# Four elementwise passes of the first norm moved from the DVE to the Pool, in a decoder layer with expert retrieval

## The chip, the cores and the metric

One core of a Trainium2 chip runs the whole kernel. The metric is device time in microseconds, the median of three runs. DVE is the vector engine, Pool is GpSimd, ACT is the scalar engine, PE is TensorE, SP issues plain DMAs.

## The reference

One decoder layer over 256 tokens of width 2048, in float32: a token mixer (recurrence and latent attention) and then an expert-retrieval feed-forward. Only the place between the two is touched:

```
x = layer_norm(DN_ALPHA * x + (1 + gt1) * mixed, ln1_g, ln1_b)   # first norm
h = x * (1 + sc2) + sh2
q = (h @ w_q)                         # 8 heads x 2 halves of 128
s = q . sub_keys; top 16 of each half; top 16 of the 16 x 16 sums -> 16 experts per token and head
act = gelu(h . expert_u[idx]) * softmax(best)
y  = sum over 8 heads x 16 experts of act * expert_v[idx]
x = layer_norm(DN_ALPHA * x + (1 + gt2) * y, ln2_g, ln2_b)
```

`expert_u` and `expert_v` have 16384 rows of 2048 floats. Each token tile of 128 tokens fetches 8 x 16 rows per token of each table.

## The kernel before, in words

Tokens lie in two tiles of 128 (T = 0, 1). After the first norm `x1[T]` holds the normalised residual without its gain and shift. Two things are derived from it on the DVE: `h2[T] = x1[T] * mods[2] + mods[1]` (the expert input, with the norm's rows folded into the two `mods` rows; lines 1775 and 1778), and the residual itself, `x1[T] = x1[T] * ln1[0] + ln1[1]` (lines 1781 and 1784; two multiplies and two additions of 128x2048). The residual is only read again by `finish(0)` and `finish(1)`, hundreds of microseconds later. PE has by then read `x1` for its transposes (semaphore `h2T_done`).

PE meanwhile multiplies with `peer_wq` in 16 weight units of four column blocks (`query_unit`), with `scores(b)` after the first unit of the next block. `scores(1)` waits until ACT has copied the queries of block 1 out of PSUM (`query(1)`), which stands on ACT behind `weigh(0, 0, 0)`, and this behind the DVE's first four dot products. The scores of head 0, tile 0, come out of the first half block early, so that the ranking can begin.

`topk(H)` on the DVE is the ranking of one head of one tile: `top_halves`, `top_pairs` (line 1741 is the 16 x 16 sum), `experts` (lines 1756, 1760, 1762 and 1764 turn ranks into row numbers; 1764 signals `topk_ok`), `expert_gates`.

The Pool issues every gather, in a written order, one indirect DMA per expert, 128 rows of 8 KB (1 MB) each. Head 0's 16 `u` gathers go to the slots in `first_u = (2, 3, 0, 1, 4, 2, 3, 5, 0, 1, 6, 4, 7, 5, 6, 7)`. Slots 0 and 1 lie where `ln1[0]` and `ln1[1]` lie, so before the change gather 2 waits until the DVE has run the four passes (`dots_done` raised by 8). Slots 4 to 7 wait for PE to be done with a weight unit (`unit_used`), a slot used again waits for its dot product (`dots_done`). Then come `first_v` (slots that lie on later weight units), and the loops of `u_group` and `v_group`, four gathers behind one small index copy (line 482): a `u` group waits for the DVE's dot products, a `v` group for PE's products (`pv_done`). The DVE's dot product of an expert is line 1807 (head 0) or 1820 (all others). It ranks head 1 after the second dot of head 0, and head 2 after the first four dots of head 1.

Of the kernel before, what the change touches and what calls it, by code (L numbers as in the profile page):

```python
# [12 lines left out]
ALU = mybir.AluOpType  # L13
# [6 lines left out]
NT = S // P  # L20
# [26 lines left out]
GROUP = 4  # L47
# [53 lines left out]
def build(nc, t, out):  # L101
    with ExitStack() as ctx:
        def sem(name):
            return ctx.enter_context(nc.semaphore(name))
# [16 lines left out]
        def at(off, n):  # L121
            return arena[:, off:off + n]
# [91 lines left out]
        x1 = [at(W + D * i, D) for i in range(NT)]  # L214
# [40 lines left out]
        ln1 = [at(R_HG, D), at(R_HG + D, D)]  # L255
# [16 lines left out]
        in_wg, in_x2, in_ln1, in_ln2, in_keys = (sem(n) for n in ("in_wg", "in_x2", "in_ln1", "in_ln2", "in_keys"))  # L272
# [24 lines left out]
            "xc_ok", "gates_done", "gates_out", "tanh_ok", "sqrt_ok", "gelu_in", "gelu_ok", "hg_ok", "in_gate_ok"))  # L297
        mod_done, mod_ok, mix_ok = (sem(n) for n in ("mod_done", "mod_ok", "mix_ok"))
        keys_t, keys_ok = sem("keys_t"), sem("keys_ok")
        var_ok, std1_ok, h2_ok, h2T_done, h2T_out = (sem(n) for n in ("var_ok", "std1_ok", "h2_ok", "h2T_done", "h2T_out"))  # L300
        sc_done, sc_out, stage_ok, best_ok, gexp_ok, topk_ok, zero_ok = (sem(n) for n in (
            "sc_done", "sc_out", "stage_ok", "best_ok", "gexp_ok", "topk_ok", "zero_ok"))
        shift_ok, norm_ok = sem("shift_ok"), sem("norm_ok")
# [2 lines left out]
        dots_done, z_ok, a_ok, diag_ok, pv_done, y_done = (sem(n) for n in ("dots_done", "z_ok", "a_ok", "diag_ok", "pv_done", "y_done"))  # L306
# [138 lines left out]
        @block.gpsimd  # L445
        def _(pool):

            me = Chain(pool, pool_s)
            pool.wait_ge(rope_ok, 1)
            for i in range(4 * KT):  # L450
                if i >= 3:
                    pool.wait_ge(mod_used, i - 2)
                pool.dma_start(ada_raw[i % 3], ada_v[:, i % KT:i % KT + 1, 2 * D + 1024 * (i // KT):2 * D + 1024 * (i // KT + 1)].rearrange("p t c -> p (t c)")  # L453
                               ).then_inc(in_ada[i % 3], 16)

            def ada_load(n, kt):
                pool.wait_ge(mod_used, n * KT + (4 * KT + kt - 3))
                pool.dma_start(ada_raw2[kt % 4], ada_v[:, kt:kt + 1, bass.ds(n * 1024 + 4 * D, 1024)].rearrange("p t c -> p (t c)")  # L458
                               ).then_inc(in_ada2[kt % 4], 16)

            pool.wait_ge(h_oout, HEADS)
            with pool.Fori(0, 4) as n:
                for kt in range(KT):
                    ada_load(n, kt)

            for e in range(TOPK):
                s = first_u[e]
                if e == 0:
                    pool.wait_ge(topk_ok, 1)
                elif s == 0 and e < 4:  # L470
                    pool.wait_ge(dots_done, 2 * GROUP)
                elif s in first_u[:e]:
                    pool.wait_ge(dots_done, 2 * GROUP + first_u.index(s) + 1)
                elif s >= 4:
                    pool.wait_ge(unit_used, 4 * B_WQ + s + 2)
                pool.indirect_dma_start(uslot[s], None, t["peer_u"][0], bass.IndirectOffsetOnAxis(arena[:, o_idx + e:o_idx + e + 1].bitcast(U32), 0)
                                        ).then_inc(in_u[s], 16)

            def index_group(ix, H, e):

                pool.sem_inc(pool_gate, 1)
                me.do(pool.tensor_copy(ix[:, e % 8:e % 8 + GROUP], arena[:, bass.ds(H * TOPK + (o_idx + e), GROUP)].bitcast(U32)))  # L482
                me.wait()
                pool.sem_inc(pool_gate, 1)

            def u_group(H, ahead, q):

                e = ahead * TOPK + q * GROUP
                if q == 0:
                    pool.wait_ge(topk_ok, H + (ahead + 1))  # L490
                pool.wait_ge(dots_done, H * TOPK + (e + GROUP))
                index_group(idxu, H, e)
                for s in range(e % 8, e % 8 + GROUP):
                    pool.indirect_dma_start(uslot[s], None, t["peer_u"][0], bass.IndirectOffsetOnAxis(idxu[:, s:s + 1], 0)).then_inc(in_u[s], 16)  # L494

            def v_group(H, q):

                e = q * GROUP
                pool.wait_ge(pv_done, H * TOPK + (e + GROUP))
                index_group(idxv, H, e)  # L500
                for s in range(e % 8, e % 8 + GROUP):
                    pool.indirect_dma_start(vslot[s], None, t["peer_v"][0], bass.IndirectOffsetOnAxis(idxv[:, s:s + 1], 0)).then_inc(in_v[s], 16)  # L502

            def first_v(s):

                pool.wait_ge(unit_used, 4 * B_WQ + (10, 12, 13, 14, 15, 16, 16, 16)[s])
                pool.indirect_dma_start(vslot[s], None, t["peer_v"][0], bass.IndirectOffsetOnAxis(arena[:, o_idx + s:o_idx + s + 1].bitcast(U32), 0)
                                        ).then_inc(in_v[s], 16)

            first_v(0)  # L510
            u_group(0, 1, 0)
            for s in (1, 2, 3):
                first_v(s)
            u_group(0, 1, 1)
            for s in (4, 5, 6, 7):
                first_v(s)
            for q in (2, 3):
                u_group(0, 1, q)
                v_group(0, q)
            last = NT * PH - 1  # L520
            with pool.Fori(1, last - 2) as H:
                me.enter(H, 1, 2 * TOPK // GROUP)
                for q in range(TOPK // GROUP):
                    u_group(H, 1, q)
                    v_group(H, q)
            me.leave(last - 3)
            u_group(last - 1, 0, 0)
            v_group(last - 2, 0)
            v_group(last - 2, 1)
            u_group(last - 1, 0, 1)  # L530
            v_group(last - 2, 2)
            u_group(last - 1, 0, 2)
            v_group(last - 2, 3)
            v_group(last - 1, 0)
            u_group(last - 1, 0, 3)
            v_group(last - 1, 1)
            u_group(last, 0, 0)
            v_group(last - 1, 2)
            v_group(last - 1, 3)
            u_group(last, 0, 1)  # L540
            v_group(last, 0)
            u_group(last, 0, 2)
            v_group(last, 1)
            u_group(last, 0, 3)
            v_group(last, 2)
            v_group(last, 3)
# [710 lines left out]
        def _(dve):  # L1257
            me = Chain(dve, dve_s)
            V = dve
            TT, TS, STT = V.tensor_tensor, V.tensor_scalar, V.scalar_tensor_tensor  # L1260
# [260 lines left out]
            for h in range(HEADS):  # L1521
                g, n = h // 4, h % 4
# [183 lines left out]
            def topk(H):  # L1706
                top_halves(H)
                top_pairs()
                experts(H)
                expert_gates(H)  # L1710
# [63 lines left out]
            for T in range(NT):  # L1774
                me.do(TT(h2[T], x1[T], mods[2], ALU.mult))
            me.wait()
            for T in range(NT):
                me.do(TT(h2[T], h2[T], mods[1], ALU.add))
            topk(0)
            for T in range(NT):  # L1780
                me.do(TT(x1[T], x1[T], ln1[0], ALU.mult))
            me.wait()
            for T in range(NT):
                me.do(TT(x1[T], x1[T], ln1[1], ALU.add))
            dve.wait_ge(h2T_out, 4)
            V.memset(zeros, 0.0).then_inc(zero_ok, 1)
            me.wait()
# [51 lines left out]
            def finish(T):  # L1839

                for c in range(4):
                    dve.wait_ge(y_done, 4 * T + c + 1)
                    cs = slice(512 * c, 512 * (c + 1))
                    me.do(TT(h2[T][:, cs], ps[:, 4 * T + c, :], mods[3][:, cs], ALU.mult))
                    me.wait()
                    me.do(STT(x1[T][:, cs], x1[T][:, cs], ALPHA, h2[T][:, cs], ALU.mult, ALU.add))
                    me.wait()
                    me.do(V.bn_stats(bn6[T][:, c, :], x1[T][:, cs]))
                if T:
                    normalized_last()  # L1850
                    return
                scale_of(T, T + 2)
                me.wait()
                for c in range(4):
                    cs = slice(512 * c, 512 * (c + 1))
                    dve.wait_ge(norm_ok, 4 * NT + 4 * T + c + 1)
                    me.do(TT(x1[T][:, cs], x1[T][:, cs], ln2[0][:, cs], ALU.mult))
                    me.wait()
                    TT(x1[T][:, cs], x1[T][:, cs], ln2[1][:, cs], ALU.add).then_inc(ln2_ok, 1)
# [9 lines left out]
            dots(PH + 1, 1, True)  # L1869
            dve.wait_ge(in_ln2, 32)  # L1870
            dve.wait_ge(mod_ok, 4)
            finish(0)
            loop(PH + 2, NT * PH - 1, 1)
            dots(NT * PH - 1, 1, False)
# [20 lines left out]
```

## Time and profile before

| | |
|---|---|
| median of 3 runs | 2408.27 us (2407.72 to 2410.21) |
| the profiled execution | 2410.57 us, its span 2408.9 us |
| PE busy | 2084.0 us (87%) |
| DVE busy | 1487.2 us (62%) |
| POOL busy | 775.6 us (32%) |
| ACT busy | 576.8 us (24%) |
| DMA queue of the Pool (gathers, and loads of w_ada) | 604.02 MB, 61.6% of 16 engines' span |

An engine's busy time says how long it had an instruction running, not that it set the pace. Where the DMA share is 1 over a long stretch, the bytes set it.

### The profile page before, as it was taken

How to read it: one execution, taken by the hardware profiler on the slowest of the kernel's cores; microseconds unless marked ns; L12 is line 12 of the kernel's file. 1: busy time of each engine (PE TensorE's matmuls, PEld its weight loads, DVE VectorE, ACT ScalarE, POOL GpSimd, SP SyncE). 2: the span in 40 equal slices, each digit the busy share in tenths (PEclk: the TensorE clock that was granted, in tenths of full speed). 3: DMA queues.
4: the chain of work that ended last, by engine and by line, in shares of the span. 5: the costliest groups of instructions: out<-in, count | busy, mean ns of one | idle time of the engine just before them, and what ended most of it. 6: DMA issues, size and time to landing. Idle time of an engine off the chain costs nothing.

```text
span 2408.9 us, 26246 instructions
## 1 busy us (share of the span) xinstructions
PE 2084.0 (87%) x9124; PEld 1428.6 (59%) x9124; DVE 1487.2 (62%) x2122; ACT 576.8 (24%) x1102; POOL 775.6 (32%) x766
## 2 busy tenths in 40 slices
PE   4899898899989999989978787877887778888887
PEld 4788798898989998878633333333333333333333
DVE  5736657657867656568665566656666765566344
ACT  1013452553334333321211111111111221111101
POOL 0000010100111000005566545554454555454662
PEclk8899899999999999999988988988898898889998
DMA  9976665754988765578999999999999999999996
GB/s 357 384 225 201 215 223 176 265 201 157 356 284 293 267 208 195 192 252 325 407 422 421 422 422 421 422 422 422 422 421 421 422 422 422 422 422 422 422 407 267
DMA packets 216162, 809.92 MB, mean 336 GB/s; under 512 B 24824, under 2 KB 45968, under 8 KB 149520
## 3 DMA queue, kind: packets, MB, share of 16 engines
q0 software_dynamic: 92160, 604.02, 61.6%
q1 hardware_dynamic: 123264, 204.11, 24.9%
q8 instruction: 55, 0.90, 0.1%
q10 hardware_dynamic: 656, 0.66, 0.1%
q14 instruction: 27, 0.22, 0.0%
HBM read 806.64 MB, written 2.10 MB: 336 GB/s over the span
## 4 chain that ended last, share of the span: by engine, by line
PE 47%; DMA 18%; DVE 15%; issue 8%; POOL 6%; ACT 4%; SPq 1%; DVEq 0%; POOLq 0%; ACTq 0%
PE ps L551 47%; DMA front<-in_peer_u,arena 13%; DVE front L1820 3%; DVE arena L1820 2%; DMA arena<-in_peer_u,arena 2%; POOL front L502 2%; DVE arena L1344 1%; POOL arena L502 1%; POOL arena L494 1%; DMA arena<-in_w_ada 1%; POOL front L494 1%; DMA front<-in_w_ada 1%; SPq L335 1%; POOL arena L482 1%; DMA arena<-in_peer_v,arena 1%
## 5 line engine op out<-in xcount | busy, mean ns | idle before, releaser
L551 PE MATMUL ps<-arena 128*128 128x512 f32 (+4 forms) x2190 | 648.7, 450 | 129.1 <-ACT arena L1170 95.1
L551 PE MATMUL ps<-front,arena 128*128 128x512 f32 (+1 forms) x1344 | 636.2, 632 | 121.9 <-ACT arena L1170 121.9
L551 PEld LDWEIGHTS ps<-arena 128*128 128x128 f32 (+1 forms) x2190 | 381.0, 201 | 384.4 <-issue 238.6
L551 PEld LDWEIGHTS ps<-front,arena 128*128 128x128 f32 x1344 | 274.6, 207 | 478.1 <-issue 354.9
L1820 DVE CUSTOM_DVE_ANT_0 arena<-arena 128x2048 f32<-128x2048 f32 x120 | 274.2, 2294 | 272.1 <-DMA arena<-in_peer_u,arena 271.8
L1820 DVE CUSTOM_DVE_ANT_0 front<-front,arena 128x2048 f32<-128x2048 f32 x120 | 274.0, 2292 | 194.8 <-DMA front<-in_peer_u,arena 193.4
L551 PE MATMUL ps<-split_f,split_ring 128*128 128x256 f32 x896 | 259.4, 290 | 0.0
L1497 DVE TENSOR_TENSOR split_ring<-front,split_pada 128x2048 fp32r<-128x2048 f32 x72 | 164.9, 2292 | 128.1 <-ACT split_pada L1077 127.7
L1158 ACT ACTIVATE arena<-arena 128x4 f32<-128x4 f32 x64 | 13.3, 207 | 960.7 <-DVE arena L1800 960.7
L453 POOL DMA_DIRECT2D arena<-in_w_ada x64 | 34.2, 535 | 517.8 <-DVEq L1409 198.6
L551 PE MATMUL ps<-arena,front 128*128 128x256 f32 (+1 forms) x864 | 190.4, 380 | 10.3 <-DVE front L1593 6.2
L482 POOL COPY arena<-arena 128x4 uint32 (+1 forms) x122 | 90.0, 738 | 334.0 <-PE ps L551 333.7
L1077 ACT ACTIVATE split_pada<-front 128x2048 fp32r<-128x2048 f32 x70 | 134.0, 1914 | 257.8 <-PE ps L551 257.8
L502 POOL DMA_INDIRECT front<-in_peer_v,arena x155 | 166.6, 1075 | 66.1 <-issue 41.0
L551 PEld LDWEIGHTS ps<-arena,front 128*128 128x128 f32 x864 | 164.6, 198 | 33.3 <-DVE front L1593 6.3
L551 PE MATMUL ps<-split_ht,split_pada 128*128 128x256 f32 x640 | 181.9, 284 | 0.0
L551 PEld LDWEIGHTS ps<-split_f,split_ring 128*128 128x128 f32 x896 | 178.4, 199 | 0.0
L494 POOL DMA_INDIRECT front<-in_peer_u,arena x120 | 151.2, 1260 | 52.1 <-issue 28.6
L494 POOL DMA_INDIRECT arena<-in_peer_u,arena x120 | 149.6, 1247 | 53.5 <-issue 28.7
L551 PEld LDWEIGHTS ps<-split_ht,split_pada 128*128 128x128 f32 x640 | 123.5, 193 | 0.0
L502 POOL DMA_INDIRECT arena<-in_peer_v,arena x93 | 108.4, 1166 | 44.0 <-POOL arena L482 25.1
L458 POOL DMA_DIRECT2D arena<-in_w_ada x64 | 33.9, 530 | 241.2 <-DVE front L1593 102.2
(259 smaller groups left out, 2892.1 us busy)
## 6 DMA issues: line engine op xcount, KB each, us to landing
front<-in_w_in SPq DMA_DIRECT2D x68, 1024.0 KB, 7.2
arena<-in_w_ada POOLq DMA_DIRECT2D x128, 512.0 KB, 6.0
front<-in_w_ada SPq DMA_DIRECT2D x64, 512.0 KB, 7.8
front<-in_w_rnn_out SPq DMA_DIRECT2D x16, 1024.0 KB, 5.6
front<-in_w_mla_out SPq DMA_DIRECT2D x16, 1024.0 KB, 5.2
front<-in_w_o SPq DMA_DIRECT2D x16, 1024.0 KB, 5.1
front<-in_peer_wq SPq DMA_DIRECT2D x13, 1024.0 KB, 6.5
arena<-in_w_ukv SPq DMA_DIRECT2D x16, 512.0 KB, 6.0
```

The lines of the kernel that those rows point to most:

```text
L335: sp.dma_start(ring[s].rearrange("p (t h c) -> p t h c", t=2, h=2)[:, :, h, :], ada_g[:, bass.ds(i * 8 + 2 * s, 2), h, j, :]).then_inc(in_ ...
L453: pool.dma_start(ada_raw[i % 3], ada_v[:, i % KT:i % KT + 1, 2 * D + 1024 * (i // KT):2 * D + 1024 * (i // KT + 1)].rearrange("p t c -> p ...
L458: pool.dma_start(ada_raw2[kt % 4], ada_v[:, kt:kt + 1, bass.ds(n * 1024 + 4 * D, 1024)].rearrange("p t c -> p (t c)")).then_inc(in_ada2[kt ...
L482: me.do(pool.tensor_copy(ix[:, e % 8:e % 8 + GROUP], arena[:, bass.ds(H * TOPK + (o_idx + e), GROUP)].bitcast(U32)))
L494: pool.indirect_dma_start(uslot[s], None, t["peer_u"][0], bass.IndirectOffsetOnAxis(idxu[:, s:s + 1], 0)).then_inc(in_u[s], 16)
L502: pool.indirect_dma_start(vslot[s], None, t["peer_v"][0], bass.IndirectOffsetOnAxis(idxv[:, s:s + 1], 0)).then_inc(in_v[s], 16)
L551: return pe.matmul(o, l, r, start=start, stop=stop, skip_group_check=True, **k)
L1077: A(whi[s % 2], ring[s], ACT.Copy).then_inc(whi_ok, 1)
L1158: me.do(A(zs[:, c0:c1], zu[:, c0:c1], ACT.Sigmoid, scale=GELU_S))
L1344: STT(part, raw, cact[:, kt:kt + 1], part, ALU.mult, ALU.add).then_inc(ada_used, 1)
L1497: TT(wlo[s], ring[s], whi[s % 2].bitcast(F32), ALU.subtract).then_inc(wlo_ok, 1)
L1820: V.tensor_tensor_reduce(uslot[s], uslot[s], h2[T], 1.0, 0.0, ALU.mult, ALU.add, zraw[:, s:s + 1]).then_inc(dots_done, 1)
```

## The change

The four passes leave the DVE. The Pool runs them ahead of its first gather, once the rows of the first norm have landed, PE has read `x1`, and the DVE has signalled the two multiplies of `h2`. The Pool waits for its own multiplies before its additions, and for its additions before gather 2 (slot 0, where `ln1[0]` lies). The DVE signals `h2_ok` twice, with one more wait for itself ahead of the ranking of head 0. `finish(0)` gets a wait for `x1_ok`.

```diff
+            pool.wait_ge(in_ln1, 32)
+            pool.wait_ge(h2T_done, 4)
+            pool.wait_ge(h2_ok, 1)
+            for T in range(NT):
+                me.do(pool.tensor_tensor(x1[T], x1[T], ln1[0], ALU.mult))
+            me.wait()
+            for T in range(NT):
+                me.do(pool.tensor_tensor(x1[T], x1[T], ln1[1], ALU.add))
             for e in range(TOPK):
                 s = first_u[e]
                 if e == 0:
                     pool.wait_ge(topk_ok, 1)
+                    pool.wait_ge(h2_ok, 2)
                 elif s == 0 and e < 4:
-                    pool.wait_ge(dots_done, 2 * GROUP)
+                    me.wait()
+                    pool.sem_inc(x1_ok, 1)
...
             for T in range(NT):
                 me.do(TT(h2[T], x1[T], mods[2], ALU.mult))
             me.wait()
+            dve.sem_inc(h2_ok, 1)
             for T in range(NT):
                 me.do(TT(h2[T], h2[T], mods[1], ALU.add))
+            me.wait()
+            dve.sem_inc(h2_ok, 1)
             topk(0)
-            for T in range(NT):
-                me.do(TT(x1[T], x1[T], ln1[0], ALU.mult))
-            me.wait()
-            for T in range(NT):
-                me.do(TT(x1[T], x1[T], ln1[1], ALU.add))
...
             dve.wait_ge(mod_ok, 4)
+            dve.wait_ge(x1_ok, 1)
             finish(0)
```

## Rows read from the trace of the kernel before

**Rows 1.** Page, DMA share in 40 equal slices of the span, in tenths.

```profile
DMA  9976665754988765578999999999999999999996
```

**Rows 2.** Windows: stretch, length, busy of PE, PEld, DVE, ACT, POOL, PEclk, DMA, GB/s.

```profile
1056.00:1070.00 14.00, 14.00 (x72) 12.43 (x71) 12.22 (x18) 0.98 (x2) 0.00 (x0) 1.00 0.07 9
1070.00:1090.00 20.00, 20.00 (x102) 17.83 (x101) 15.86 (x31) 3.78 (x7) 1.96 (x2) 1.00 0.98 348
1090.00:1094.00 4.00, 4.00 (x20) 3.53 (x19) 3.87 (x5) 0.00 (x0) 3.05 (x1) 1.00 0.24 92
1094.00:1146.00 52.00, 52.00 (x258) 46.19 (x257) 43.29 (x82) 9.23 (x28) 33.45 (x21) 1.00 0.89 339
1146.00:1188.00 42.00, 40.89 (x156) 27.98 (x156) 28.79 (x61) 10.72 (x27) 20.16 (x17) 1.00 1.00 411
1188.00:1250.00 62.00, 53.59 (x136) 25.14 (x135) 35.76 (x67) 10.79 (x33) 48.21 (x39) 0.89 1.01 416
1250.00:2330.00 1080.00, 877.13 (x1789) 371.41 (x1788) 638.07 (x1097) 175.26 (x559) 573.29 (x532) 0.89 1.01 421
```

**Rows 3.** DVE timeline: start, duration, line and operation, [idle before it, its releaser].

```profile
1063.79 4.50 DVE L1778 TENSOR_TENSOR arena<-arena,front 128x2048 f32<-128x2048 f32 x2
1068.20 0.48 DVE L1721 MAX8 arena<-arena 128x8 f32<-128x128 f32 x2
...
1071.54 0.40 DVE L1741 TENSOR_TENSOR arena<-arena 128x256 f32<-128x256 f32 x1
...
1076.12 0.69 DVE L1756 TENSOR_TENSOR arena<-arena 128x512 f32<-128x512 f32 x1
1076.85 0.69 DVE L1760 TENSOR_TENSOR arena<-arena 128x512 f32<-128x512 f32 x1
...
1078.30 0.18 DVE L1764 SCALAR_TENSOR_TENSOR arena<-arena 128x16 uint32<-128x16 f32 x1
...
1081.31 4.49 DVE L1781 TENSOR_TENSOR arena<-arena 128x2048 f32<-128x2048 f32 x2
...
1090.59 2.29 DVE L1807 CUSTOM_DVE_ANT_0 front<-front,arena 128x2048 f32<-128x2048 f32 x1
...
1095.02 0.48 DVE L1721 MAX8 arena<-arena 128x8 f32<-128x128 f32 x2
...
1139.66 2.29 DVE L1807 CUSTOM_DVE_ANT_0 arena<-arena 128x2048 f32<-128x2048 f32 x1 [3.14 <-DMA arena<-in_peer_u,arena]
```

**Rows 4.** DVE timeline, one dot product of a later head.

```profile
1267.09 2.29 DVE L1820 CUSTOM_DVE_ANT_0 arena<-arena 128x2048 f32<-128x2048 f32 x1 [4.80 <-DMA arena<-in_peer_u,arena]
```

**Rows 5.** POOL timeline, gathers and one index copy, same columns.

```profile
1078.75 0.99 POOL L476 DMA_INDIRECT front<-in_peer_u,arena  x1 [250.98 <-DVE arena L1764]
...
1090.65 3.05 POOL L476 DMA_INDIRECT arena<-in_peer_u,arena  x1 [9.64 <-DVEq L1788]
...
1153.28 1.26 POOL L507 DMA_INDIRECT front<-in_peer_v,arena  x1 [6.79 <-PE ps L551]
...
1188.34 2.20 POOL L502 DMA_INDIRECT arena<-in_peer_v,arena  x1 [0.81 <-POOL arena L482]
...
1267.10 2.33 POOL L482 COPY arena<-arena 128x4 uint32 x1
```

**Rows 6.** Source line 476, the gather issued at 1090.65 alone, issue to landing.

```profile
L476 POOL DMA_INDIRECT arena<-in_peer_u,arena x1: 3049/3049/3049, 1090.6 to 1090.6; - x1
...
DMA to landing us min/median/max: 7.5/7.5/7.5
```

**Rows 7.** Source line 507, the gather issued at 1153.28 alone, issue to landing.

```profile
L507 POOL DMA_INDIRECT front<-in_peer_v,arena x1: 1265/1265/1265, 1153.3 to 1153.3; - x1
...
DMA to landing us min/median/max: 8.0/8.0/8.0
```

**Rows 8.** ACT timeline, the copy of the queries of block 1 out of PSUM.

```profile
1111.41 1.00 ACT L1147 ACTIVATE arena<-ps 128x1024 f32<-128x1024 f32 x1
```

**Rows 9.** PE timeline, weight units 7 and 8, scores(1), unit 9.

```profile
1100.92 22.67 PE L551 MATMUL ps<-arena 128*128 128x256 f32 x112
```

More of the change, by code:

```diff
@@ L299, in build @@
         keys_t, keys_ok = sem("keys_t"), sem("keys_ok")
-        var_ok, std1_ok, h2_ok, h2T_done, h2T_out = (sem(n) for n in ("var_ok", "std1_ok", "h2_ok", "h2T_done", "h2T_out"))
+        var_ok, std1_ok, h2_ok, x1_ok, h2T_done, h2T_out = (sem(n) for n in ("var_ok", "std1_ok", "h2_ok", "x1_ok", "h2T_done", "h2T_out"))
         sc_done, sc_out, stage_ok, best_ok, gexp_ok, topk_ok, zero_ok = (sem(n) for n in (
```

## The prediction

> **What bounds the kernel now.** I read the page's slices first: the DMA row stands at 9 tenths without a break from the 23rd slice, some 1325 us, to the last but one [rows 1]. So the second half of the kernel, the expert phase, is not paced by an engine. The windows put a sharper edge on it [rows 2]. Between 1056 and 1070 us the DMA share is 0.07, between 1090 and 1094 it is 0.24, between 1094 and 1146 it is 0.89. From 1146 on it is 1.00 or 1.01, at 411, 416 and 421 GB/s, for nearly 1200 us. From there the time to the end is bytes over rate: 128 rows of 8 KB are 1.049 MB, at 421 GB/s 2.49 us a gather. An edit ahead of 1146 us counts for what it does to the moment at which this full stretch begins, and for nothing else. Of the whole stretch only its first 42 us give anything back: 411 against 421 GB/s are about 1.0 us of room.
>
> What sets that moment is read from the DVE timeline [rows 3]. The `h2` additions end at 1068.2, the ranking of head 0 signals its row numbers at 1078.5, the four passes take 1081.31 to 1090.3, two dots follow from 1090.59, the ranking of head 1 starts at 1095.02. From there the DVE has work without a gap worth naming until the last dot of head 0 waits 3.14 us for its gather, at 1139.66. Gathers on slots used again wait for those dots, so a shift of the ranking of head 1 travels down the whole chain, into the first gathers of head 1. I call it D.
>
> **What is removed.** The four passes, 2 x 4.49 us by the row of the first pair, 9.28 us from 1081.31 to the first dot at 1090.59 [rows 3]. They stand on D's path. They are also what the gathers into slots 0 and 1 wait for: gather 2 is issued at 1090.65 [rows 5].
>
> **What is added.** Four Pool passes of 128x2048 on two inputs. Everything the Pool has to issue is queued behind them, above all gather 0, which was issued 0.45 us after the DVE's last ranking step began (1078.75 against 1078.30). Two prices are unknown.
>
> First, the length of a pass, p. No row has such an operation on the Pool. Below, the DVE's 2.29 us for the same elements (half of 4.49, plus the overlap) [rows 3]. Above, a Pool instruction that handles 128 rows takes 0.99 us, 7.7 ns a row [rows 5]; at that pace 2048 columns are 15.8 us. The nearer row is the DVE's, and I take twice that, 4.58 us, as for an engine that fetches its two inputs one after the other. The Trainium skill, page "GPSIMD Engine Reference", section "Elementwise — side-by-side cycle accounting", gives a tensor_tensor of 2048 float32 as 4497 ns on the Pool against 2293 ns on the DVE; no run here shows the former, the trace agrees with the latter (2.29). With it the sum below would be 0.3 us less.
>
> Second, whether the two engines can run together. The Pool's index copy of 4 elements, issued at 1267.10 beside a dot that runs 1267.09 to 1269.38, takes 2.33 us and ends at 1269.43 [rows 4, 5]. Gather 2, at 1090.65 beside the first dots, takes 3.05 us instead of 0.99, so it ends some 0.8 us behind the dot that it met [rows 3, 5]. So a Pool instruction that touches the memory waits until the DVE's two-input instruction has ended. How the DVE fares when the Pool was first no row shows, since the Pool never holds anything for long. Bounds: the DVE loses nothing, or it waits out each pass. I take the second: whichever starts first keeps the path for the whole instruction, and they take turns. Then the passes are not beside the ranking, but between its steps.
>
> That turn-taking, by these rows. The `h2` multiplies end at 1063.79 and release the Pool; the DVE's first addition already runs, to 1066.08. Pass 1: 1066.08 to 1070.66. Second addition, held until then: to 1072.95. Pass 2: to 1077.53. The ranking begins at 1072.95 instead of 1068.20; its one-input steps run freely. The 16 x 16 sum (two inputs) is due 3.34 us later, 1076.29, is held to 1077.53 and ends at 1077.93. Pass 3: to 1082.51. Line 1756 is due 4.58 us after the sum began, 1082.11, is held to 1082.51, ends at 1083.20. Pass 4: to 1087.78. Line 1760 is held until then, and line 1764 starts 1.45 us after it: 1089.23, against 1078.30 before. The ranking is 10.9 us late.
>
> Gather 0 is issued 0.45 us later, 1089.68. It takes 0.99 us and lands 4.45 us after its end (7.5 less 3.05 in [rows 6]): 1095.12. Gather 1 lands one transfer later, 1097.60; its dot takes 2.21 us more. The ranking of head 1 starts at 1099.8 instead of 1095.02: **D = +4.8 us**. So 9.3 us are taken off the path, and 10.9 us of later ranking plus about 3.2 us of gather latency, which the four passes used to cover, are put on it. Gathers 2 and 3 are issued at about 1092 and 1093 (before: 1090.65 and 1094.0) and are landed by 1105; the dots that need them come at 1110.
>
> **A new wait on PE.** `scores(1)` needs ACT's copy of block 1, which ended at 1112.41 [rows 8], behind the DVE's first four dots. PE reaches it after two weight units, 64 of the 112 instructions that begin at 1100.92 [rows 9]; the 96 large ones take 0.217 us, so it is there at 1114.8. Now the copy ends at 1117.2, and PE stalls 2.4 us. The gates that PE sets for the Pool move by as much: the `v` gather of 1153.28, for which the Pool idled 6.79 us, and that of 1188.34 [rows 5]. Both move less than D, so neither makes the DMA idle. This costs nothing more.
>
> The rest: the DVE's extra wait ahead of the ranking and the signals, at most 0.2 us; each hand-over between the engines a little more, unknown, below 0.2 us by the 0.05 us that the copy of [rows 5] ended behind the dot, about 0.8 in four turns at most. `finish(0)`'s wait costs nothing: the passes are done hundreds of microseconds earlier.
>
> **Sum.** D 4.8, hand-overs and the extra wait 0 to +1.0, room in the 42 us behind 1146 0 to -1.0: +4.8, with +3.5 to +6.5 around it. Against the profiled execution (span 2408.9 plus 1.7 us around it, 2410.57) that is 2415.4. That execution is 2.3 us above the median of the runs, 2408.27, so the forecast for the median is 2413.1.
>
> **Rivals.**
> *Passes longer than 4.58 us, with turn-taking.* Each microsecond on p adds 4 to D; 6 us make +10.5, 2418.8. The Trainium skill, page "GPSIMD Engine Reference", section "Instruction dispatch", also says that a kernel's first call on the Pool can cost about 6 us of code loading; no row here shows a first call that is long. Such a load would lie beside the DVE's additions and cost well under its length.
>
> *No turns: the DVE is not held.* For it: no row shows the DVE held. Against it: the Pool is. The ranking ends at 1078.5, the Pool's passes at 1063.9 + 4 x 4.58 = 1082.2. Gather 0 lands at 1087.7, gather 1 at 1090.2, the ranking of head 1 starts at 1092.4: D = -2.6. But little of it would be kept. The `v` gather of 1153.28 stays where PE puts it. It ended at 1154.54 and landed at 1161.3 [rows 5, 7], against 1159.0 with an empty queue, so the DMA can run at most some 2.3 us ahead there before it idles, perhaps 3.5 if the index copy behind it is quicker. Result 2406. This is the rival on the other side, faster, though hardly by a measurable step. The Trainium skill, page "SBUF — State Buffer", section "SBUF: two separate sides", speaks against it: the Pool and a DVE instruction with two SBUF inputs share a port pair under an exclusive lock, and the one that comes second blocks for the whole instruction. The trace agrees for the Pool as second; the other order no run shows yet.
>
> *Turns, but short passes.* With p = 2.29 the same working has the sum held to 1075.3, line 1764 at 1082.1 and gather 1 landed at 1090.5: D = -2.3, and 2406.3. The change decides at p near 3.1 us: below it gains, above it loses.
>
> *The shift is absorbed.* The windows before 1146 have 5.7 us of idle DMA (0.89 of 52 us). Should the dots of head 0 catch up, for instance by gathers 2 to 7 that now land well ahead, the full stretch starts as before: 2408.5. Against it: those dots run back to back, so they can't catch up.
>
> **Chances.** A difference under 0.2%, 4.8 us, can't be told from none. Forecast 0.56, of which 0.43 above that bound and 0.13 below it; longer passes 0.10, slower; absorbed 0.10, the same; no turns 0.14, of which 0.03 faster; short passes 0.10, of which 0.02 faster. Slower 0.43 + 0.10 = 0.53, faster 0.05, same 0.42. The range reaches over both small gains, whose 2406 has error too, and over most of the longer passes: 2405.5 to 2418.5. The likeliest case alone has 2411.8 to 2414.8.
>
> **What would show it.** Four Pool passes near 4.5 us, none overlapping a two-input DVE step; the second `h2` addition, line 1741, and lines 1756 or 1760 late or long by what is left of a pass; line 1764 near 1089; gather 0 near 1090 and a DVE idle of some 5 us ahead of the first dot; the ranking of head 1 near 1100; a PE gap ahead of `scores(1)`; the DMA share full from about 1150. It is wrong if the ranking ends near 1078.5, if the passes overlap it, or if the DMA's full stretch begins no later.

## The result, and the profile after

The changed kernel takes 2413.53 us (median of 15 runs, 2410.79 to 2416.29), the one before 2407.97 us (15 runs, 2406.23 to 2410.21). The ratio is 1.0023, with a 95% interval of 1.0015 to 1.0031: slower by 5.6 us. The forecast was 2413.1, the loss put at 4.8 us. The profiled execution took 2413.96 us, its span is 2412.2.

In this execution the first `h2` multiplication begins at 1058.17 us, in that of before at 1059.27. The 1.1 us come from upstream of the change, where the code is the same. Below, "offset" is the time since that start. Line numbers of the changed kernel lie 10 or 11 higher for the rows of [rows 3], for instance 1764 is now 1774.

The DVE's timeline of the changed kernel (start, duration, line and operation, [idle before, releaser]), against [rows 3]:

```profile
1062.80 8.81 DVE L1789 TENSOR_TENSOR arena<-arena,front 128x2048 f32<-128x2048 f32 x2
1071.87 0.49 DVE L1731 MAX8 arena<-arena 128x8 f32<-128x128 f32 x2 [0.26 <-DVE arena L1789]
...
1075.21 1.06 DVE L1751 TENSOR_TENSOR arena<-arena 128x256 f32<-128x256 f32 x1
1076.31 4.38 DVE L1754 CAST arena<-arena 128x32 f32<-128x32 uint32 x1
...
1083.79 1.38 DVE L1761 TENSOR_SCALAR arena<-arena 128x16 uint32<-128x16 uint32 x1
...
1085.50 0.69 DVE L1766 TENSOR_TENSOR arena<-arena 128x512 f32<-128x512 f32 x1
...
1087.67 0.18 DVE L1774 SCALAR_TENSOR_TENSOR arena<-arena 128x16 uint32<-128x16 f32 x1
...
1093.79 2.29 DVE L1815 CUSTOM_DVE_ANT_0 front<-front,arena 128x2048 f32<-128x2048 f32 x1 [5.47 <-DMA front<-in_peer_u,arena]
1097.22 2.29 DVE L1815 CUSTOM_DVE_ANT_0 front<-front,arena 128x2048 f32<-128x2048 f32 x1 [1.13 <-DMA front<-in_peer_u,arena]
1099.43 0.48 DVE L1731 MAX8 arena<-arena 128x8 f32<-128x128 f32 x2
...
1143.78 2.29 DVE L1815 CUSTOM_DVE_ANT_0 arena<-arena 128x2048 f32<-128x2048 f32 x1 [2.89 <-DMA arena<-in_peer_u,arena]
```

The Pool's timeline of the same execution, against [rows 5]:

```profile
1062.89 13.10 POOL L470 TENSOR_TENSOR arena<-arena 128x2048 f32<-128x2048 f32 x2 [236.24 <-DVEq L1787]
1076.07 9.07 POOL L473 TENSOR_TENSOR arena<-arena 128x2048 f32<-128x2048 f32 x2
1088.12 1.01 POOL L486 DMA_INDIRECT front<-in_peer_u,arena  x1 [2.99 <-DVE arena L1774]
...
1157.19 1.63 POOL L517 DMA_INDIRECT front<-in_peer_v,arena  x1 [3.86 <-PE ps L561]
...
1192.58 2.52 POOL L512 DMA_INDIRECT arena<-in_peer_v,arena  x1 [0.82 <-POOL arena L492]
```

Read the two together. A start is the moment at which an instruction was handed to its engine, so the duration of one that was held includes its wait. The two additions of `h2` took 4.50 us in [rows 3] and take 8.81 here. The first runs 1062.80 to 1065.09 and the Pool, dispatched at 1062.89, waits for it; the second is held for a Pool pass. The 16 x 16 sum takes 1.06 instead of 0.40, a cast of 32 elements 4.38 us where others take 0.18, a tensor-scalar step on 16 elements 1.38 where others take 0.18. The sum ends at 1076.27, 0.28 us past the first pair of passes at 1075.99, and the tensor-scalar step at 1085.17, 0.03 past the second pair at 1085.14. The cast ends at 1080.69, where one of the two passes between is over. From 1076.27 to 1085.14 the Pool does two passes with no more than the cast between them, 4.43 us each. The steps with MAX8 keep their 0.49.

So the ranking begins at offset 13.7 instead of 8.9, gives its row numbers at 29.5 instead of 19.0, and the ranking of head 1 begins at 41.3 instead of 35.8: D = +5.5.

The windows of the changed kernel (columns as in [rows 2]):

```profile
1070.00:1090.00 20.00, 20.00 (x102) 17.83 (x101) 16.51 (x38) 3.78 (x7) 16.63 (x5) 1.00 0.76 246
1090.00:1094.00 4.00, 4.00 (x21) 3.51 (x20) 0.21 (x1) 0.00 (x0) 2.90 (x4) 1.00 0.91 334
1094.00:1146.00 52.00, 48.92 (x227) 42.85 (x226) 45.93 (x80) 8.17 (x23) 27.67 (x16) 0.97 0.82 318
1146.00:1188.00 42.00, 40.89 (x173) 29.87 (x172) 28.86 (x66) 11.79 (x32) 26.32 (x20) 1.00 0.99 406
1250.00:2330.00 1080.00, 873.81 (x1785) 369.88 (x1784) 638.04 (x1102) 175.35 (x557) 563.21 (x533) 0.89 1.01 422
```

Against [rows 2], the DMA's share falls from 0.98 to 0.76 in the first stretch and from 0.89 to 0.82 in the third, and rises in the short one. By share times length, from 1070 to 1146 it idles 4.8 + 0.4 + 9.4 = 14.6 us instead of 0.4 + 3.0 + 5.7 = 9.1: some 5.5 us more, and from 1056 to 1070 it idles 0.7 less (share 0.12 instead of 0.07), since this execution is 1.1 us ahead. At the end it is 4.4 us later by offset, the medians are 5.6 apart. Behind 1250 us the share is the same.

PE's new gap stands ahead of `scores(1)` in PE's timeline:

```profile
1116.88 10.62 PE L561 MATMUL ps<-arena 128*128 128x128 f32 x48 [3.08 <-ACT arena L1157]
```

The gap costs PE more than its 3.08 us. Behind it the granted clock of TensorE, 1.00 before, falls to 0.50, which is the lower of its two levels (1.2 instead of 2.4 GHz), and is back at 1.00 from 1122 us. A window in between:

```profile
1119.00:1121.00 2.00, 2.00 (x7) 1.71 (x7) 2.00 (x3) 0.00 (x0) 1.69 (x2) 0.50 0.85 332
```

The 48 multiplications take 10.62 us; in the kernel before they are the last of the row of [rows 9] and take 8.7 (22.67 less 13.98 for the first 64, as the changed kernel has them). So PE is 5.0 us late behind them. The `v` gathers that wait for PE go at offset 99.0 and 112.8 instead of 94.0 and 107.8, and the first `v` group begins at 133.4 instead of 128.1.

### The profile page after: what moved, and what is told of

Read it like the earlier page. It is cut to its first block, busy times and chain, and to the rows that moved or that the text cites. A ratio compares the mean times of both kernels' runs of the same rounds, so it can differ in the third digit from the quotient of the medians.

```text
span 2412.2 us, 26266 instructions
## 1 busy us (share of the span) xinstructions
PE 2081.3 (86%) x9124; PEld 1427.0 (59%) x9124; DVE 1489.2 (62%) x2118; ACT 576.4 (24%) x1102; POOL 786.0 (33%) x770
## 4 chain that ended last, share of the span: by engine, by line
PE 46%; DMA 21%; DVE 12%; issue 8%; POOL 7%; ACT 4%; SPq 1%; POOLq 0%; DVEq 0%; ACTq 0%
PE ps L561 46%; DMA front<-in_peer_u,arena 11%; DMA arena<-in_peer_u,arena 5%; POOL front L512 2%; DVE arena L1828 2%; DVE front L1828 2%; DMA arena<-in_peer_v,arena 2%; DMA front<-in_w_ada 1%; POOL arena L512 1%; POOL front L504 1%; POOL arena L504 1%; DVE arena L1354 1%; DMA arena<-in_w_ada 1%; POOL arena L492 1%; SPq L335 1%
## 5 line engine op out<-in xcount | busy, mean ns | idle before, releaser
L492 POOL COPY arena<-arena 128x4 uint32 (+1 forms) x122 | 84.1, 689 | 346.2 <-PE ps L561 345.8
L504 POOL DMA_INDIRECT front<-in_peer_u,arena x120 | 144.4, 1203 | 52.1 <-issue 28.6
```

## The experiments

Each was run against the kernel before on the same chip. The table gives shifts in us against the kernel before, each from one profiled execution and counted from the first `h2` multiplication: D of the ranking of head 1, the 129th dot product (halfway through), the end of the span; then the ratio of the runs with its interval. e1, e3, e5 and e6 shared the runs of the kernel before (median 2408.44 us), as did e2, e4, e7 and e8 (2408.26), and e9 to e11 (2408.37).

| | D | 129th dot | end | ratio (95% interval) |
|---|---|---|---|---|
| the change | +5.5 | +4.9 | +4.4 | 1.0023 (1.0015 to 1.0031) |
| e1 no passes | -3.0 | -0.2 | -0.2 | 1.0002 (0.9993 to 1.0011) |
| e2 half width | +2.0 | -0.1 | 0.0 | 1.0004 (0.9995 to 1.0013) |
| e3 behind gathers | +4.5 | +6.7 | +5.4 | 1.0034 (1.0022 to 1.0046) |
| e4 writes only | -0.9 | -0.2 | -0.1 | 0.9995 (0.9986 to 1.0004) |
| e5 query first | +5.7 | +4.8 | +4.5 | 1.0023 (1.0014 to 1.0032) |
| e6 two more on DVE | +4.5 | +3.1 | +2.4 | 1.0007 (0.9998 to 1.0016) |
| e7 cast late | 0.0 | 0.0 | -0.6 | 0.9999 (0.9990 to 1.0008) |
| e8 two passes each | -3.8 | -0.5 | -0.3 | 1.0000 (0.9991 to 1.0009) |
| e9 order, two passes | -3.7 | -5.2 | -5.6 | 0.9976 (0.9966 to 0.9985) |
| e10 order alone | 0.0 | -1.1 | -1.9 | 0.9994 (0.9985 to 1.0003) |
| e11 order, no passes | -3.0 | -5.3 | -5.4 | 0.9983 (0.9974 to 0.9992) |

The executions start the first `h2` multiplication between 1056.0 and 1059.5 us, though all kernels are the same up to there, so the first three columns tell mechanisms apart better than the whole times do. Each of them is one execution; the ends agree with the differences of the medians within 1.4 us.

### e3: the passes beside the dots

```diff
-            for T in range(NT):
-                me.do(pool.tensor_tensor(x1[T], x1[T], ln1[0], ALU.mult))
-            me.wait()
-            for T in range(NT):
-                me.do(pool.tensor_tensor(x1[T], x1[T], ln1[1], ALU.add))
             for e in range(TOPK):
...
                 elif s == 0 and e < 4:
+                    for T in range(NT):
+                        me.do(pool.tensor_tensor(x1[T], x1[T], ln1[0], ALU.mult))
+                    me.wait()
+                    for T in range(NT):
+                        me.do(pool.tensor_tensor(x1[T], x1[T], ln1[1], ALU.add))
                     me.wait()
                     pool.sem_inc(x1_ok, 1)
```

> The change with the four Pool passes moved behind gathers 0 and 1, so that they lie beside the first dots and the ranking of head 1. Turn-taking: the ranking of head 0 is on time, its row numbers some 10 us earlier than in the change; but the first two dots are each held by a pass, the passes end near 1103 us of the span, gather 2 comes there, and the third dot is 4 to 6 us later than before: 4 to 6 us above before. Rival, that the Pool's passes only delay what is queued behind them on the Pool and do not hold the DVE: the passes end near 1099, the third dot is on time, and the kernel is within 1 us of before.

2415.27 us, the slowest of all. The ranking of head 0 is on time (offset 19.1), so the lateness in the change does come from the passes that lie beside it. The DVE's timeline shows the first two dots, 2.29 us each otherwise, and the sum in the ranking of head 1:

```profile
1085.05 6.12 DVE L1815 CUSTOM_DVE_ANT_0 front<-front,arena 128x2048 f32<-128x2048 f32 x1 [5.45 <-DMA front<-in_peer_u,arena]
1091.10 6.59 DVE L1815 CUSTOM_DVE_ANT_0 front<-front,arena 128x2048 f32<-128x2048 f32 x1
...
1100.96 1.40 DVE L1751 TENSOR_TENSOR arena<-arena 128x256 f32<-128x256 f32 x1
```

and the Pool's the passes and the gather behind them:

```profile
1079.99 9.02 POOL L476 TENSOR_TENSOR arena<-arena 128x2048 f32<-128x2048 f32 x2
1089.09 12.99 POOL L479 TENSOR_TENSOR arena<-arena 128x2048 f32<-128x2048 f32 x2
1102.89 0.97 POOL L486 DMA_INDIRECT arena<-in_peer_u,arena  x1 [0.81 <-POOL arena L479]
```

The second dot is 6.59 us long: its own 2.29 and nearly a whole pass. That rules out the rival in which the passes only queue up on the Pool. The third dot came 5.7 us late by offset, the middle of what was expected. The whole time, 6.8 us above the median of before, is above the 4 to 6 expected.

### e4: Pool instructions that only write

```diff
-            for T in range(NT):
-                me.do(pool.tensor_tensor(x1[T], x1[T], ln1[0], ALU.mult))
-            me.wait()
-            for T in range(NT):
-                me.do(pool.tensor_tensor(x1[T], x1[T], ln1[1], ALU.add))
+            for T in 4 * (0, 1):
+                me.do(pool.memset(x1[T], 1.0))
+                me.wait()
```

> The change with the four Pool passes replaced by eight Pool memsets of 128x2048, which read nothing (the residual is overwritten with 1). If a Pool instruction that only writes holds the DVE's two-input steps too, the second h2 addition and the 16 x 16 sum are late as in the change. If only reading holds them, those two run on time, and only the copies and tensor-scalar steps of the ranking can be held. With memsets of about 2.2 us, 17 to 18 us in all, the first case gives a ranking 5 us or more late and 1 to 5 us above before; the second a ranking 0 to 3 us late and -2 to +1 us. Where they differ is in the DVE rows.

The Pool's timeline and the DVE's beside it:

```profile
1060.78 14.84 POOL L470 MEMSET arena<- 128x2048 f32 x8 [236.19 <-DVEq L1785]
```

```profile
1060.72 4.49 DVE L1787 TENSOR_TENSOR arena<-arena,front 128x2048 f32<-128x2048 f32 x2
...
1068.81 0.41 DVE L1749 TENSOR_TENSOR arena<-arena 128x256 f32<-128x256 f32 x1
1069.26 0.82 DVE L1752 CAST arena<-arena 128x32 f32<-128x32 uint32 x1
...
1073.06 0.14 DVE L1755 TENSOR_SCALAR arena<-arena 128x1 f32<-128x1 f32 x1
1073.18 0.61 DVE L1759 TENSOR_SCALAR arena<-arena 128x16 uint32<-128x16 uint32 x1
1073.26 0.55 DVE L1760 TENSOR_SCALAR arena<-arena 128x16 uint32<-128x16 uint32 x1
1073.85 1.81 DVE L1762 CAST arena<-arena 128x32 f32<-128x32 uint32 x1
```

The eight memsets end at 1075.62, 1.86 us each with the wait between them. Beside them the two-input additions and the two-input sum take what they always take (4.49 and 0.41). The casts and the tensor-scalar steps of 16 elements, which have one input, are held: 0.82 and 1.81 instead of 0.18, 0.61 and 0.55 instead of 0.17. The tensor-scalar of one element is not (0.14), and neither was it beside a pass in the change. So there are two holds. A Pool instruction that reads two tiles holds both kinds; one that only writes holds the one-input casts and tensor-scalars alone. The second case of the expectation holds. The kernel took 2407.04 us, 1.2 below before.

### e2: passes of half the width

```diff
-                me.do(pool.tensor_tensor(x1[T], x1[T], ln1[0], ALU.mult))
+                me.do(pool.tensor_tensor(x1[T][:, 0:1024], x1[T][:, 0:1024], ln1[0][:, 0:1024], ALU.mult))
```

(and the additions in the same way)

> The change with each of the four Pool passes over 1024 instead of 2048 columns (the other half of the residual then lacks gain and shift). A pass was 4.4 us; now some 2.2. Turn-taking with the same working as in the prediction: the ranking of head 0 is about 4 us later than before instead of 10.5, D is about -2: 1 to 3 us below before. Rival, that the loss comes from something that does not scale with the passes (the extra wait, the new signals, a first call on the Pool): still 4 us or more above before.

2409.20 us, 0.9 above before, where I expected 1 to 3 below. The row numbers came 5.2 us late (offset 24.2), not 10.5, so the loss scales with the passes and is not that of a signal or a first call. But D was +2.0 where I expected -2. Gather 0 landed as reckoned, at offset 30.4; gather 1 only at 35.5, 5.1 us behind it, where I had one transfer of 2.5. In the change that step is 3.4 us. In both, gathers 2 and 3 are issued right behind, and in e2 the load of weight unit 15 falls into the same stretch; in the kernel before, gather 1 landed 8.9 us after its issue under the DVE's passes, so that its delay did not show. What shares the DMA with gather 1 I have not taken apart.

### e5: without PE's stall

```diff
-            weigh(0, 0, 0)
             query(1)
+            weigh(0, 0, 0)
```

> The change with one swap on ACT: the copy of the queries of block 1 ahead of the first four weights, so that the 3.1 us stall of PE ahead of scores(1) goes. My theory: that stall costs nothing, since the gathers' bytes set the end: within 1 us of the change, 5 to 6 us above before. Rival, that the stall is part of the loss: 2 to 3 us below the change.

2413.43 us, against 2413.53 of the change. The stall of 3.08 us and the slower clock behind it cost nothing: the two `v` gathers go at offset 94.0 and 107.8 again, as in the kernel before, and the end is the same. The third gate is not tested by this. PE now waits 3.91 us for ACT some 50 us later, so the first `v` group still begins at 132.7. That this one costs nothing either rests on the DMA's share alone: 1.01 in the 43 us before offset 130, 1.00 in the 60 us behind it.

### e6: a later ranking of head 1, without the Pool

```diff
                 me.do(TT(x1[T], x1[T], ln1[1], ALU.add))
+            me.wait()
+            for T in range(NT):
+                me.do(TT(x1[T], x1[T], x1[T], ALU.max))
```

> The kernel before with two more passes of 128x2048 on the DVE behind the four (each tile's maximum with itself, which changes nothing), no Pool pass. They delay the ranking of head 1 by 4.5 us and hold the DVE nowhere else. My theory, that the start of the DMA's full stretch sets the end one for one: 3.5 to 5 us above before. Rival, that such a delay is absorbed later: within 1 us of before.

2409.88 us, 1.4 above the 2408.44 of before, with an interval that includes no change. D is +4.5 to the tenth and the last dot of head 0 is 4.5 late, but halfway only 3.1 are left and at the end 2.4. Neither theory: a shift of the full stretch is not passed on one for one, some 1.5 us are given back halfway. In e2 +2.0 becomes nothing, in the change +5.5 becomes +4.9. So what is given back is between 0.6 and 2.0 us, and differs from kernel to kernel.

### e1: no passes at all

```diff
-            for T in range(NT):
-                me.do(pool.tensor_tensor(x1[T], x1[T], ln1[0], ALU.mult))
-            me.wait()
-            for T in range(NT):
-                me.do(pool.tensor_tensor(x1[T], x1[T], ln1[1], ALU.add))
...
                 elif s == 0 and e < 4:
-                    me.wait()
                     pool.sem_inc(x1_ok, 1)
```

> The change with its four Pool passes left out (the residual then lacks the first norm's gain and shift). My theory: the ranking of head 0 ends as in the kernel before, gather 1 has landed 7.7 us after its first issue or so, and the ranking of head 1 starts about 3.9 us earlier than before (D = -3.9); but PE's gate on the fourth v gather lets the DMA run only some 2.3 to 3.5 us ahead, so 1.5 to 3.5 us below the kernel before. Rival, that the 9.3 us of passes stood fully on the path: 9 us below. Rival, that the later end of the changed kernel has nothing to do with the passes: still 4 to 6 us above before.

2407.66 against 2408.44 us, ratio 1.0002. Even with the work left out there is nothing to gain. The ranking of head 1 began 3.0 us early and the last dot of head 0 ran 3.0 us early; the third group of head 1 was only 0.6 ahead and the fourth 0.6 behind. I had expected 1.5 to 3.5 us to be left. With no passes the ranking of head 0 began at offset 9.4 instead of 8.9, so the extra wait and the signals alone cost 0.45 us.

### e7 and e8: half of the work moved, and where it fits

e7 moves the cast of the indices behind the second top 16, in every ranking:

```diff
                 me.wait()
-                me.do(V.tensor_copy(topf, topi))
                 hold()
                 top16(pairs)
...
                 me.do(V.tensor_copy(rankf, ranki))
+                me.do(V.tensor_copy(topf, topi))
```

> The kernel before with the ranking's cast of the candidate indices moved from ahead of the second top 16 to behind it, in every ranking; a control for the next one. Nothing is held in the kernel before, so within 0.7 us of it.

2408.19 against 2408.26 us: no change, as a control should have it. e8 has the same, and

```diff
+            pool.wait_ge(in_ln1, 32)
+            pool.wait_ge(h2T_done, 4)
+            pool.wait_ge(h2_ok, 2)
+            for T in range(NT):
+                me.do(pool.tensor_tensor(x1[T], x1[T], ln1[0], ALU.mult))
+            me.wait()
+            pool.sem_inc(x1_ok, 1)
...
             topk(0)
-            for T in range(NT):
-                me.do(TT(x1[T], x1[T], ln1[0], ALU.mult))
-            me.wait()
+            dve.wait_ge(x1_ok, 1)
             for T in range(NT):
                 me.do(TT(x1[T], x1[T], ln1[1], ALU.add))
```

> Only the two multiplications on the Pool, started behind the h2 additions, with the cast moved as in the one before so that the second pass lies beside one-input steps; the two additions stay on the DVE behind the ranking. Turn-taking: pass 1 holds the 16 x 16 sum by some 1.2 us, pass 2 a tensor-scalar step by 0.8; the DVE's own passes are 4.5 us shorter; the ranking of head 1 starts 1.5 to 2.5 us earlier than before: 1 to 2.5 us below before. Rival, that the DVE is held for longer or in other steps than two-input and wide one-input ones: at or above before.

Its DVE and Pool timelines:

```profile
1069.17 1.45 DVE L1748 TENSOR_TENSOR arena<-arena 128x256 f32<-128x256 f32 x1
...
1073.76 1.27 DVE L1757 TENSOR_SCALAR arena<-arena 128x16 uint32<-128x16 uint32 x1
```

```profile
1065.82 9.18 POOL L470 TENSOR_TENSOR arena<-arena 128x2048 f32<-128x2048 f32 x2 [240.91 <-DVEq L1788]
...
1150.46 0.93 POOL L514 DMA_INDIRECT front<-in_peer_v,arena  x1 [7.76 <-PE ps L558]
...
1164.27 1.44 POOL L514 DMA_INDIRECT front<-in_peer_v,arena  x1 [5.94 <-PE ps L558]
...
1184.52 0.38 POOL L489 COPY arena<-arena 128x4 uint32<-128x4 uint32 x1 [8.69 <-PE ps L558]
```

In the kernel before, behind the gather of 1153.28 [rows 5]:

```profile
1167.10 0.94 POOL L507 DMA_INDIRECT front<-in_peer_v,arena  x1 [4.02 <-PE ps L551]
...
1187.34 0.19 POOL L482 COPY arena<-arena 128x4 uint32<-128x4 uint32 x1 [6.19 <-PE ps L551]
```

The holds are 1.05 and 1.1 us (1.2 and 0.8 expected) and the ranking is 2.2 us late for two passes of 4.5 us, which now do lie beside it; 0.45 of it is the extra wait. D is -3.8, where I expected -1.5 to -2.5. And 2408.40 us against 2408.26: again nothing arrives at the end, where I expected 1 to 2.5. The Pool's rows tell where it went. Its three gates open at offset 94.0, 107.8 and 128.1 in both kernels, since PE keeps its pace, and the Pool stands before them for 7.76, 5.94 and 8.69 us instead of 6.79, 4.02 and 6.19.

### e9, e10, e11: the order of the gathers

```diff
-            for s in (1, 2, 3):
+            for s in (1, 2):
                 first_v(s)
             u_group(0, 1, 1)
-            for s in (4, 5, 6, 7):
+            for s in (3, 4):
                 first_v(s)
-            for q in (2, 3):
-                u_group(0, 1, q)
-                v_group(0, q)
+            u_group(0, 1, 2)
+            for s in (5, 6, 7):
+                first_v(s)
+            u_group(0, 1, 3)
+            for q in (2, 3):
+                v_group(0, q)
```

e9 is e8 with it, e10 the kernel before, e11 e1.

> The kernel with two multiplications on the Pool and two additions on the DVE, whose ranking of head 1 began 3.8 us earlier and whose end did not move, now with the Pool's written order changed behind the first v gathers: a u group whose slots are free goes ahead of each v gather that still waits for PE. My theory: the 3.8 us were lost while the Pool stood at PE's gates with u gathers ready behind them; with those ahead, 2 to 4 us below before. Rival, that the floor is elsewhere (the gate of the first v group behind PE's first products): within 1 us of before.

> The kernel before with the new gather order alone. Its DMA has no idle time to speak of at those gates, so my theory has it within 1 us of before; should it gain more than 1 us, the order itself is worth something and the one above is not the sum of an earlier ranking and an open gate.

> The change without its four passes (the residual then lacks the first norm's gain and shift) and with the new gather order. Its ranking of head 1 began 3.0 us earlier than before and nothing of it reached the end. Theory: with the gates passed by, 2 to 3.5 us below before. Rival as above: within 1 us.

e9 takes 2402.40 us against 2408.37, ratio 0.9976 (0.9966 to 0.9985), the fastest of all and faster than both kernels. e11 takes 2403.81, e10 2407.31. Halfway through, the order alone is worth 1.1 us, and e8 without it 0.5; together they are 5.2. So the 3.8 us that e8 wins ahead of the gates arrive once the gates are passed by. The windows just around the gates, first of e8, then of e9:

```profile
1140.00:1190.00 50.00, 48.89 (x189) 33.12 (x189) 34.54 (x67) 10.72 (x27) 20.36 (x19) 1.00 0.95 384
```

```profile
1140.00:1190.00 50.00, 48.89 (x188) 32.92 (x187) 35.96 (x73) 12.95 (x36) 37.84 (x26) 1.00 1.00 411
```

At 384 GB/s the DMA of e8 moves 19.2 MB in these 50 us, at 411 that of e9 20.6: 1.35 MB more, which take 3.2 us at the rate of the full stretch. The rival, no gain because the floor is at the first `v` group, falls as a forecast. But the new order also puts the last `u` group of head 1 ahead of that gate, so the share of each gate is not told apart. e9 and e11 gained more than I had written (6.0 and 4.6 us by the medians), about 1 us of it by the order itself. Beyond the order's own 1.1 us, e11 is 4.2 ahead halfway with a lead of 3.0, so the two parts do not add up to the microsecond.

## Why the prediction was right, point by point

**The bound.** Right: behind 1250 us the DMA's share is 1.01 in all thirteen kernels, and the 5.5 us that it idles more from 1070 to 1146 are of the size of the loss, 4.4 us by offset in that execution and 5.6 in the medians. One reading was off: the page's DMA row [rows 1] stands at 9 from its 20th slice, some 1144 us, and not from the 23rd. The forecast went by the windows, which say 1146.

**The length of a pass**, 4.58 us: 4.43 measured in the change, 4.54 in e3 where nothing held it. **Turn-taking**: right, and shown by e3 in which a dot is held for a pass. The Trainium skill, page "SBUF — State Buffer", section "SBUF: two separate sides", has the DVE's two-port modes held by any Pool instruction, and its two-input instructions only by one that reads: e4 agrees for the additions, free beside memsets (4.49 us), and for the casts and tensor-scalars held (up to 1.81 us), if these ran in such a mode, which no run here shows.

**The working of the ranking.** The start was put at 4.75 us late and was 4.8; its end at 10.9 and was 10.5. The held steps were not all the ones that I named. I had lines 1756 and 1760 wait for passes 3 and 4; it was the cast in front of the second top 16 (4.38 us), and a tensor-scalar step (1.38), behind which the Pool was done. I had counted one-input steps as free; two kinds of them are not. The total is close by two errors of opposite sign, which is luck: the Pool's passes ended at offset 27.0, 1.5 us before the 28.5 of the working, but 2.5 us of the ranking were left behind them instead of 1.45. The hand-overs and the extra wait, 0 to 1.0 us in the sum, are within these 10.5; e1 has the wait and the signals at 0.45, where I allowed 0.2.

**Gather 0**, landed at 1095.1 by the forecast: offset 35.85, measured 35.6. **Gather 1** one transfer later: mis-sized, 3.4 us instead of 2.5. These 0.9 us less the 0.2 of gather 0 are the difference between D = 4.8 and 5.5.

**PE's stall**: 2.4 forecast, 3.08 measured. I had PE's gates move by the stall alone; with the lower clock behind it (0.50) they moved by 5.0, 5.0 and 5.3 us. That is still less than the 5.5 of D, so the conclusion stood, by a narrow margin. e5 shows it for the first two gates.

**From D to the end.** The step was "one for one, room 0 to 1.0". For the change it held (5.5 to 4.9 halfway). As a rule it was wrong: e6 gives back 1.4 of 4.5 us, e2 all of 2.0. On the other side it was wrong by more: the rivals without turns and with short passes were to reach 2406, and e1, e4 and e8, which started the ranking of head 1 between 0.9 and 3.8 us early, all stayed within 0.1% of before. I had priced the gate at the `v` gather of 1153.28 alone; the one at 1167 and that of the first `v` group at 1188 come behind it, and each takes more of the lead. The point from which the change would gain, p near 3.1, was not found: e2, with passes of 2.4 us, was level. Its D was +2.0 where the same working has -2.3, mostly by 1.4 us of later row numbers and 2.6 of a later gather 1.

The windows show how much is won back or lost behind the ranking. These run over the 103 us from offset 87.0 to 190.0, in the order of the kernel before, the change, e2 and e8:

```profile
1146.27:1249.27 103.00, 93.47 (x288) 52.59 (x287) 63.88 (x125) 20.67 (x58) 67.68 (x55) 0.93 1.00 413
1145.17:1248.17 103.00, 93.00 (x314) 54.81 (x313) 61.69 (x114) 21.19 (x62) 71.17 (x56) 0.98 1.00 413
1144.41:1247.41 103.00, 92.73 (x287) 52.19 (x286) 63.40 (x122) 20.62 (x57) 70.05 (x57) 0.93 1.01 419
1143.44:1246.44 103.00, 93.12 (x287) 52.29 (x286) 59.59 (x122) 20.67 (x58) 58.94 (x55) 0.93 0.98 400
```

At 421 GB/s, e2 moves what takes 1.5 us more than in the kernel before, and so makes up most of its 2.0; the change moves the same as before and keeps its loss; e8 moves 3.2 us less, nearly its whole lead. So the room is 1.5 us where I had at most 1.0. I had looked for it in the first 42 us only, and by [rows 2] the next 62 run at 416 GB/s, which is 0.7 us more. Why the change takes nothing of this room is open.

The loss of the changed kernel has thus three terms by the rows: 10.5 us of later row numbers; 4.3 us of landing of gathers 0 and 1 (until offset 39.0), which the four passes used to cover and which I had put at 3.2; and 9.3 us taken off. They make the 5.5 of D.

## What to carry to other kernels

In these traces a tile pass moved from the DVE to the Pool lay beside the DVE's work only where that work had neither two inputs nor was a cast or tensor-scalar; elsewhere it stood in series with it, at twice the length, so look at each instruction it will meet, and place it beside the others (e8: two passes for 2.2 us). Ask what a removed stretch was covering: here 9.3 us of passes covered the landing of two gathers, and without them the next step began only 3.0 us earlier. And when an edit gains ahead of a saturated resource and the end does not move, look for the next in-order queue that stands at another engine's gate with ready work behind it; here a lead of 3.0 to 3.8 us stood behind such gates, and one reordering let it out (e9, e11).

## What the runs showed of the hardware

- A Pool tensor_tensor of 128x2048 float32 takes 4.4 to 4.5 us, a memset of that size 1.80 us. The first call of the former showed no extra time in e3, where it began right behind the record of a change of the Pool's configuration: its first two passes have 4.541 and 4.545 us. The 13.10 us of the first pair in the change are, by an estimate from the DVE's 2.2 to 2.3 us an addition, two passes of 4.3 and two waits.

```profile
L476 POOLq MODIFY_POOL_CONFIG  x2: 48/48/48, 1079.9 to 1079.9; - x2
L476 POOL TENSOR_TENSOR arena<-arena x2: 4541/4543/4545, 1080.0 to 1084.5; 128x2048 f32<-128x2048 f32 x2
```

- A cast of 128x32 elements, 0.18 us by itself, took 4.38 us where it met a Pool pass, and 1.81 beside a memset. MAX8, FIND_INDEX8 and MATCH_REPLACE8 kept their durations beside the same passes.
- The engines took turns: the sum that had waited ended at 1076.27, the Pool's third pass, handed over at 1076.07, went next, and the cast, handed over at 1076.31, waited for it.
- TensorE's granted clock fell from 1.00 to 0.50 for some 3.5 us behind a gap of 3.08 us in which PE did nothing, and PE lost 1.9 us more by it.
